# Loading the token records of an expert one expert later, ahead of its weights instead of behind them

## The chip, the cores and the metric

The kernel runs on one core of one Trainium2 chip. The time is the device time of one execution in microseconds (us), the median of the runs named. TensorE (PE) multiplies matrices, VectorE (DVE) and ScalarE (ACT) work element by element, GpSimd (POOL) gathers and scatters rows, and SyncE (SP) issues most transfers. Every transfer, whoever issues it, is moved by the same 16 DMA engines.

## The reference

One layer of a diffusion backbone over 2048 tokens of width 1024: a modulated RMSNorm, an input projection into windowed attention and a gated long convolution, an output projection, and then a mixture of 32 experts. Only that last part is touched. Each token goes to the two best experts of its best group:

```
e_val, e_idx = lax.top_k(jax.nn.softmax(e_logits, axis=-1), TOP_K)
gate = g_val * e_val / jnp.sum(e_val, axis=-1, keepdims=True)
expert = g_idx * EXPERTS_PER_GROUP + e_idx
...
def expert_block(args):
    xb, e = args
    return (jax.nn.silu(xb @ exp_w1[e]) * (xb @ exp_w3[e])) @ exp_w2[e]
...
out = jnp.zeros((n_tok, d), h.dtype).at[tok_sorted].add(y)
```

Each expert has w1 and w3 of 1024x512 and w2 of 512x1024 in float32, 2 MB each, so 6 MB per expert and 192 MB in all.

## The kernel before

The stages before the experts (normalisation, projection, convolution, attention, output projection, router) take the first two thirds of the time. The router stage writes a table in HBM: for each expert, one record (token number and gate) per token that chose it.

`stage6` then goes through the experts 0 to 31 in order. An expert's first 128 tokens are its *main* step (`main`); tokens beyond 128 go in *lots* of 32 (`lot`), which come before the main step. How many there are is read at run time: `span` (L2522, L2523) loads, from the small table `info` in SBUF (part of the tile `lead`), the number of steps of an expert (`many`) and the number of lots before it (`lots`). The steps are numbered through: step n works on record column n of the tile `rec` (`brec`).

Who does what in an expert:

- SP loads w1 and w3 (`load13`, issued at L2557 of the helper, two DMAs of 2 MB into `lead` or `raw`, by parity of the expert), w2 (`load2`, L2561, 2 MB into `w`), and the records (`records`, L2767 for a lot and L2769 for the main step, 1 KB each). All of these go through SP's one hardware queue.
- POOL gathers the token rows of step n+2 during step n: it copies the record column (L2718) and issues the indirect gather into `xg` (L2721). It waits for that record and for PE's transposes of the step (L2813), since `xg` is a single buffer. At the end of a step it adds the results into the output (L2739, for a lot L2730).
- ACT and DVE split the weights of the *next* expert into a high and a low float32r half while PE multiplies with those of this one. ACT's copy of the first quarter of the next w3 (L2645, `w3h`) stands ahead of its copies of the transposed gated values (`gTh`, L2676), for which PE waits before its output product (L2875).
- PE multiplies: L2825 and L2843 in a lot, L2857, L2858, L2863 (hidden), L2875, L2879, L2886 (output) in a main step.

SP's program is one ordered list. In `records` each record waits for the landing of the one before it (`rl` counts them), also for the last; it does not wait for its own landing. `load13` of expert ex+2 waits until the lots of ex are through the first product (`lhm`) and until the low halves of ex have been made (`lo`); `load2` of ex+2 waits for the last output product of ex (`ym`).

Of the kernel before, what the change touches and what calls it, by code (L numbers as in the profile page):

```python
# [42 lines left out]
NE = 32  # L43
# [2386 lines left out]
def stage6(e, g):  # L2430
# [10 lines left out]
    with e.stage(clear=True) as st:  # L2441
# [79 lines left out]
        def span(eng, ex):  # L2521
            many = eng.value_load(info[0:1, 0, bass.ds(ex, 1)], min_val=1, max_val=MANY)  # L2522
            lots = eng.value_load(info[0:1, 1, bass.ds(ex, 1)], min_val=0, max_val=TILES - NE)  # L2523
            return many, lots
# [30 lines left out]
        def load13(eng, ex, par, m):  # L2555
            src = i[("exp_w1", "exp_w3")[m]][0, bass.ds(ex, 1)].rearrange("a (k p) f -> p (a k) f", p=P)
            eng.dma_start(raw13[par][:, m, :, :], src).then_inc(ldw13[m][par], 16)  # L2557

        def load2(eng, ex, par):
            src = i["exp_w2"][0, bass.ds(ex, 1)].rearrange("a (k p) f -> p (a k) f", p=P)  # L2560
            eng.dma_start(w2[par][:, :, :], src).then_inc(ldw2[par], 16)  # L2561
# [193 lines left out]
        @block.sync  # L2755
        def _(sp):
            for b in range(2):
                for m in range(2):
                    sp.sem_inc(ldw13[m][b], 16)
            sp.sem_inc(ldw2[0], 16)  # L2760

            def records(ex, many, lots):
                with sp.If(many > 1):
                    with sp.Fori(0, many - 1) as b:
                        sp.wait_ge(rl, 16 * (lots + ex + b + 1))
                        lot = g.table[bass.ds(ex * CAP + P + b * LOT, LOT), :].unsqueeze(0).broadcast_to([GR, LOT, 2])
                        sp.dma_start(rec[:, bass.ds(lots + ex + b, 1), :].rearrange("p a b -> p (a b)"), lot).then_inc(rl, 16)  # L2767
                sp.wait_ge(rl, 16 * (lots + ex + many))
                sp.dma_start(rec[:, bass.ds(lots + ex + many - 1, 1), :], g.table[bass.ds(ex * CAP, P), :].unsqueeze(1))\  # L2769
                  .then_inc(rl, 16)  # L2770
            first, second, third = span(sp, 0), span(sp, 1), span(sp, 2)
            sp.wait_ge(blank, 1)
            sp.wait_ge(g.last_records, 32)
            sp.sem_inc(passed_s, 1)
            sp.sem_inc(rl, 16)
            sp.sem_inc(lhm, 1)
            records(0, *first)
            records(1, *second)
            records(2, *third)
            sp.wait_ge(g.second_w2, 16)  # L2780
            sp.sem_inc(ldw2[1], 16)

            def next_weights(ex, par, more=True):
                many, lots = span(sp, ex)
                sp.wait_ge(lhm, lots + many)
                sp.sem_inc(passed_s, 1)
                for m in range(2):
                    sp.wait_ge(lo[m], PARTS * (ex + 1))
                    sp.sem_inc(passed_s, 1)
                    load13(sp, ex + 2, par, m)  # L2790
                if more:
                    records(ex + 3, *span(sp, ex + 3))
                sp.wait_ge(ym, 2 * ex + 2)
                sp.sem_inc(passed_s, 1)
                load2(sp, ex + 2, par)
            with sp.Fori(0, NE // 2 - 2) as pair:
                next_weights(2 * pair, 0)
                next_weights(2 * pair + 1, 1)
            next_weights(NE - 4, 0)
            next_weights(NE - 3, 1, False)  # L2800

            total = sp.value_load(info[0:1, 2, NE - 1:NE], min_val=0, max_val=TILES - NE) + NE
            for k in range(2):
                sp.wait_ge(rl, 16 * (total + k + 1))
                sp.dma_start(rec[:, bass.ds(total + k, 1), :], g.table[NE * CAP:NE * CAP + P, :].unsqueeze(1)).then_inc(rl, 16)
# [207 lines left out]
```

## Time and profile before

| what | value |
|---|---|
| median of 3 runs | 2409.44 us (2406.88 to 2416.59) |
| the profiled execution's own time | 2416.59 us, its span 2414.8 us |
| PE busy | 2232.1 us, 92% of the span |
| DVE, ACT, POOL busy | 59%, 51%, 21% |
| DMA | 414.01 MB, mean 171 GB/s |
| the experts' stage | about 1605 to 2415 us of the span |

The profile gives for each engine how long it was busy and what ended its idle time. For SP, "busy" means nothing: what matters there is when it issues each transfer and what it waits for. Views used: waits (who waited for whom), windows (busy time, granted PE clock and DMA share of a stretch), the timeline of one engine, the chain of waits (the work that ended last), and the DMA issues with the time from issue to landing.

### The profile page before, as it was taken

The numbers are of one execution on the slowest core, as the hardware profiler recorded it, in microseconds if no ns is written. First come the engines' busy times: TensorE is split into PE (matmuls) and PEld (weight loads), VectorE is DVE, ScalarE is ACT, GpSimd is POOL, SyncE is SP. The second block draws the span as 40 slices with busy tenths as digits, with TensorE's granted clock in tenths as the row PEclk, the third lists the DMA queues.
The fourth block names the chain that finished last, engine by engine and source line by source line (L and its number), as shares of the span: only waits on it lengthen the run. The fifth ranks groups of instructions, "written<-read, shape, count | busy, mean of one in ns | idle before, by whom it ended". The sixth has DMA issues, their size and how long they took to land. (4 is left out here: it accounts for less than half of the span.)

```text
span 2414.8 us, 43573 instructions
## 1 busy us (share of the span) xinstructions
PE 2232.1 (92%) x15189; PEld 1553.4 (64%) x15190; DVE 1432.3 (59%) x2489; ACT 1232.0 (51%) x2144; POOL 498.3 (21%) x770
## 2 busy tenths in 40 slices
PE   5998999999979999789999999849899999999998
PEld 2335777888846666456666666637666776666775
DVE  4456686232325555555555555448677887666886
ACT  4556322222134444455555555237577777566774
POOL 2672111000011101001222222232222122222122
PEclk8898999999989999899999999969999999999999
DMA  8894222222283542612222221368987998887994
GB/s 295 276 283 137 61 53 78 61 79 70 70 218 91 126 109 73 187 55 62 80 66 79 62 70 62 125 212 291 308 307 256 370 309 292 285 259 238 326 326 150
DMA packets 241969, 414.01 MB, mean 171 GB/s; under 512 B 25572, under 2 KB 129260, under 8 KB 236772
## 3 DMA queue, kind: packets, MB, share of 16 engines
q1 hardware_dynamic: 197904, 354.24, 44.7%
q0 software_dynamic: 18800, 44.71, 7.6%
q10 hardware_dynamic: 25125, 13.18, 2.0%
q8 instruction: 90, 1.47, 0.3%
q14 instruction: 50, 0.40, 0.1%
HBM read 344.83 MB, written 76.85 MB: 175 GB/s over the span
## 5 line engine op out<-in xcount | busy, mean ns | idle before, releaser
L937 PE MATMUL ps_proj<-sb_hTh,sb_winh 128*128 128x512 f32 x576 | 234.0, 406 | 5.4 <-DVE sb_hTl L1089 2.7
L939 PE MATMUL ps_proj<-sb_hTh,sb_winl 128*128 128x512 f32 x576 | 225.2, 391 | 0.0
L938 PE MATMUL ps_proj<-sb_hTl,sb_winh 128*128 128x512 f32 x576 | 225.0, 391 | 0.0
L2237 DVE CUSTOM_DVE_ANT_0 sb_lead<-ps_S,sb_mask 128x640 f32<-128x640 f32 x124 | 102.0, 823 | 88.4 <-PE ps_S L1966 81.9
L2120 ACT ACTIVATE sb_lead<-sb_lead,sb_nm 128x640 f32<-128x640 f32 x128 | 106.3, 830 | 80.2 <-DVE sb_nm L2241 79.0
L1062 ACT COPY sb_rope_or_conv<-ps_proj 128x512 f32<-128x512 f32 x48 | 28.3, 589 | 219.2 <-PE ps_proj L939 144.9
L937 PEld LDWEIGHTS ps_proj<-sb_hTh,sb_winh 128*128 128x128 f32 x576 | 108.7, 189 | 33.4 <-issue 4.1
L2114 ACT COPY sb_lead<-ps_PT 128x512 f32<-128x512 f32 x160 | 89.4, 580 | 74.4 <-PE ps_PT L1958 74.3
L2739 POOL DMA_INDIRECT out<-sb_by,sb_rows_out x32 | 73.2, 2287 | 254.4 <-issue 240.4
L938 PEld LDWEIGHTS ps_proj<-sb_hTl,sb_winh 128*128 128x128 f32 x576 | 108.6, 188 | 25.6 <-issue 4.1
L939 PEld LDWEIGHTS ps_proj<-sb_hTh,sb_winl 128*128 128x128 f32 x576 | 108.6, 188 | 23.3
L1565 DVE TENSOR_TENSOR sb_ab<-sb_ab,ps_gp 128x1024 f32<-128x1024 f32 x64 | 75.3, 1218 | 73.0 <-PE ps_gp L1372 73.0
L1945 PE MATMUL ps_S<-sb_kT,sb_qb 64*128 64x384 f32 x248 | 117.7, 556 | 0.4 <-DVE sb_mx L2237 0.4
L2886 PE MATMUL ps_byp<-sb_w,sb_gT 128*128 128x512 f32 x256 | 115.0, 592 | 0.0
L1145 DVE TENSOR_SCALAR sb_rope_or_conv<-sb_rope_or_conv,sb_cols 128x2048 f32<-128x2048 f32 x11 | 14.8, 1346 | 163.8 <-ACT sb_rope_or_conv L1062 163.8
L2857 PE MATMUL ps_bh<-sb_w1h,sb_bxh 128*128 128x512 f32 x256 | 109.7, 428 | 0.0
L2005 PE MATMUL ps_M<-sb_woh,sb_mixh 128*128 128x512 f32 x256 | 103.9, 406 | 2.0 <-DVE sb_mixl L2323 2.0
L1966 PE MATMUL ps_S<-sb_kT,sb_qb 64*128 64x256 f32 x248 | 90.0, 444 | 16.3 <-DVE sb_mx L2237 11.0
L2609 DVE TENSOR_TENSOR sb_w1l<-sb_w,sb_w1h 128x1024 fp32r<-128x1024 f32 x64 | 75.6, 1222 | 46.7 <-ACT sb_w1h L2682 46.7
L2007 PE MATMUL ps_M<-sb_woh,sb_mixl 128*128 128x512 f32 x256 | 101.3, 396 | 0.0
L2858 PE MATMUL ps_bh<-sb_w1l,sb_bxh 128*128 128x512 f32 x256 | 101.2, 395 | 0.0
L2857 PE MATMUL ps_bh<-sb_w3h,sb_bxh 128*128 128x512 f32 x256 | 101.1, 395 | 0.0
(354 smaller groups left out, 5590.0 us busy)
## 6 DMA issues: line engine op xcount, KB each, us to landing
sb_lead<-in_exp_w SPq DMA_DIRECT2D x32, 2048.0 KB, 14.4
sb_w<-in_exp_w SPq DMA_DIRECT2D x32, 2048.0 KB, 9.1
sb_raw<-in_exp_w SPq DMA_DIRECT2D x32, 2048.0 KB, 14.7
sb_ada<-in_ada_w SPq DMA_DIRECT2D x16, 1536.0 KB, 8.1
scr_filt<-sb_fout SPq DMA_DIRECT2D x128, 128.0 KB, 3.2
sb_yh<-scr_filt SPq DMA_DIRECT2D x64, 256.0 KB, 5.0
scr_hy_in<-sb_hcT ACTq DMA_DIRECT2D x12, 1024.0 KB, 5.5
sb_win<-in_w_in SPq DMA_DIRECT2D x9, 1024.0 KB, 6.0
```

Source lines behind the costliest of these rows:

```text
L937: pe.matmul(mp[:, r % 4, 0:N], a, high[:, k, :], start=(k == 0), stop=False)
L938: pe.matmul(mp[:, r % 4, 0:N], a, low[:, k, :], start=False, stop=False)
L939: ins = pe.matmul(mp[:, r % 4, 0:N], b, high[:, k, :], start=False, stop=(k == KT - 1))
L1945: return pe.matmul(mixer_local if tile.n == 0 and p % 2 else local_of[p % 2], qb[tile.par][0:HD, order[p], :], g.kT[0:HD, order[p] // 4, b ...
L1966: context = pe.matmul(mixer_context if alone and p % 2 else context_of[p % 2], qb[nx.par][HD:2 * HD, order[p], :], g.kT[HD:2 * HD, order[p ...
L2005: pe.matmul(M[:, half, :], mixh[:, k, :], woh[:, k, cs], start=(k == 0), stop=False)
L2007: ins = pe.matmul(M[:, half, :], mixl[:, k, :], woh[:, k, cs], start=False, stop=(k == KT - 1))
L2120: act.activation(pr[:, p, :], pr[:, p, :], ACT.Exp, bias=nm[:, nx.par, p:p + 1], scale=SCALE, accum_out=rsum[:, nx.par, p:p + 1]).then_inc ...
L2237: ve.tensor_tensor_reduce(out=pr[:, p, :], in0=mixer_scores if nx.n == 0 and p % 2 else scores_of[p % 2], in1=mask[:, edge, mask_of[p % 2] ...
L2857: pe.matmul(hp[:, m, :], xh[:, k, :], high[m][:, k, :], start=(k == 0), stop=False)
L2858: pe.matmul(hp[:, m, :], xh[:, k, :], low[m][:, k, :], start=False, stop=False)
L2886: ins = pe.matmul(yp[:, part, :], gT[:, f - SPLIT, :], w2[par][:, f, part * 512:(part + 1) * 512], start=False, stop=(f == FT - 1), skip_g ...
```

## The change

Before, three experts' records were loaded ahead of the loop, and within the turn for expert ex the records of ex+3 were loaded after `load13(ex+2)` and ahead of `load2(ex+2)`. Now two experts' records are loaded ahead of the loop, and the turn for ex begins with the records of ex+2, so that they stand behind `load2(ex+1)` of the turn before and ahead of `load13(ex+2)`. The last two turns, written out after the loop before, are in the loop now.

```diff
-            first, second, third = span(sp, 0), span(sp, 1), span(sp, 2)
+            first, second = span(sp, 0), span(sp, 1)
...
             records(1, *second)
-            records(2, *third)
             sp.wait_ge(g.second_w2, 16)
             sp.sem_inc(ldw2[1], 16)
 
-            def next_weights(ex, par, more=True):
+            def next_weights(ex, par):
+                records(ex + 2, *span(sp, ex + 2))
                 many, lots = span(sp, ex)
                 sp.wait_ge(lhm, lots + many)
                 sp.sem_inc(passed_s, 1)
@@
                     load13(sp, ex + 2, par, m)
-                if more:
-                    records(ex + 3, *span(sp, ex + 3))
                 sp.wait_ge(ym, 2 * ex + 2)
                 sp.sem_inc(passed_s, 1)
                 load2(sp, ex + 2, par)
-            with sp.Fori(0, NE // 2 - 2) as pair:
+            with sp.Fori(0, NE // 2 - 1) as pair:
                 next_weights(2 * pair, 0)
                 next_weights(2 * pair + 1, 1)
-            next_weights(NE - 4, 0)
-            next_weights(NE - 3, 1, False)
```

On SP's list, in the first half of the loop's body, the kernel before has (L2557 is `load13`, L2522 and L2523 read `many` and `lots`, L2767 and L2769 are the records, L2561 is `load2`):

```order
L2557 DMA sb_lead<-in_exp_w1 128x8x512
L2557 DMA sb_lead<-in_exp_w3 128x8x512
L2522 ISA
L2522 TENSOR_LOAD sb_lead
L2522 ISA x2
L2523 ISA
L2523 TENSOR_LOAD sb_lead
L2523 ISA x2
L2763 COMPARE_AND_BRANCH
```

and, after the records of the lots (L2764 is their loop):

```order
L2764 COMPARE_AND_BRANCH
L2763 UNCONDITIONAL_BRANCH
L2768 ISA
L2769 ISA
L2769 REGISTER_ALU
L2769 DMA sb_brec<-scr_table 128x2
L2793 ISA
L2561 DMA sb_w2_0<-in_exp_w2 128x4x1024
```

In the change the same body, from the end of the records on, reads:

```order
L2769 DMA sb_brec<-scr_table 128x2
L2522 ISA
L2522 TENSOR_LOAD sb_lead
L2522 ISA x2
L2523 ISA
L2523 TENSOR_LOAD sb_lead
L2523 ISA x2
L2785 REGISTER_ALU
L2788 ISA
L2557 ISA
L2557 DMA sb_lead<-in_exp_w1 128x8x512
L2557 DMA sb_lead<-in_exp_w3 128x8x512
```

The records have moved from between w3 and w2 to ahead of w1, and between the last record and the next weight load there now stand the two reads of `info`, where before nothing stood but the wait for `ym`. The lists of the other engines keep their order.

## Rows read from the trace of the kernel before

**Rows 1.** Waits, SP from 1600, PE from 1620 us: total us, times, longest.

```profile
SPq L2769 <- DMA sb_brec<-scr_table: 101.5, 16, 12.9
SPq L2767 <- DMA sb_brec<-scr_table: 47.5, 6, 12.1
...
PE ps_btp L2813 <- DMA sb_xg<-scr_xn,sb_rows_in: 10.0, 5, 3.1
```

**Rows 2.** Windows: length, busy of PE, PEld, DVE, ACT, POOL, clock, DMA share, GB/s.

```profile
1699.10:1723.10 24.00, 21.27 (x82) 15.11 (x81) 18.21 (x28) 15.29 (x24) 2.89 (x3) 0.93 0.87 300
1890.10:1909.40 19.30, 19.23 (x83) 14.02 (x81) 16.76 (x26) 13.45 (x21) 4.99 (x3) 1.00 1.04 369
1948.00:1967.80 19.80, 19.73 (x86) 13.99 (x86) 17.33 (x27) 15.23 (x24) 2.88 (x3) 1.00 0.81 273
1683.50:1690.50 7.00, 7.00 (x32) 5.63 (x31) 5.46 (x6) 4.38 (x5) 3.74 (x1) 1.00 0.42 66
1715.00:1718.50 3.50, 3.50 (x11) 2.77 (x12) 2.75 (x8) 2.43 (x8) 0.00 (x0) 0.60 0.78 234
```

**Rows 3.** The chain of waits, 1650 to 1740 us: start, us, what.

```profile
1669.59 15.04 DMA sb_brec<-scr_table
1684.93 2.90 DMA sb_brec<-scr_table
...
1692.55 20.92 DMA sb_raw<-in_exp_w
...
1729.53 7.58 DMA sb_xg<-scr_xn,sb_rows_in
```

**Rows 4.** SP's timeline around expert 5's records: start, us, what.

```profile
1661.18 0.38 SPq L2561 DMA_DIRECT2D sb_w<-in_exp_w  x1
...
1688.13 0.37 SPq L2769 DMA_DIRECT2D sb_brec<-scr_table  x1
1688.77 0.39 SPq L2561 DMA_DIRECT2D sb_w<-in_exp_w  x1
1691.98 4.20 SPq L2557 DMA_DIRECT2D sb_raw<-in_exp_w  x2
```

**Rows 5.** SP's timeline around expert 15's records.

```profile
1934.88 0.38 SPq L2561 DMA_DIRECT2D sb_w<-in_exp_w  x1
1937.30 4.85 SPq L2557 DMA_DIRECT2D sb_raw<-in_exp_w  x2
```

**Rows 6.** w3 of experts 15, 19, 31: SP's issue, then the us to landing.

```profile
1937.85 4.29 SPq L2557 DMA_DIRECT2D sb_raw<-in_exp_w  x1
sb_raw<-in_exp_w SPq DMA_DIRECT2D x1, 2048.0 KB, 20.2
...
2037.52 2.40 SPq L2557 DMA_DIRECT2D sb_raw<-in_exp_w  x1
sb_raw<-in_exp_w SPq DMA_DIRECT2D x1, 2048.0 KB, 20.7
...
2349.91 3.81 SPq L2557 DMA_DIRECT2D sb_raw<-in_exp_w  x1
sb_raw<-in_exp_w SPq DMA_DIRECT2D x1, 2048.0 KB, 19.3
```

**Rows 7.** ACT's timeline: first quarter of w3 of experts 5, 15, 19, 31.

```profile
1713.55 1.04 ACT L2645 CAST sb_w3h<-sb_raw 128x1024 fp32r<-128x1024 f32 x1 [3.89 <-DMA sb_raw<-in_exp_w]
...
1959.79 1.05 ACT L2645 CAST sb_w3h<-sb_raw 128x1024 fp32r<-128x1024 f32 x1 [1.23 <-PE ps_bh L2863]
...
2060.23 1.05 ACT L2645 CAST sb_w3h<-sb_raw 128x1024 fp32r<-128x1024 f32 x1 [1.14 <-PE ps_bh L2863]
...
2370.42 1.05 ACT L2645 CAST sb_w3h<-sb_raw 128x1024 fp32r<-128x1024 f32 x1 [1.23 <-PE ps_bh L2863]
```

**Rows 8.** w2 of expert 3, us to landing; POOL's pick of expert 4's record.

```profile
sb_w<-in_exp_w SPq DMA_DIRECT2D x1, 2048.0 KB, 12.3
...
1673.72 0.18 POOL L2718 COPY sb_rows_in<-sb_brec 128x1 int32 x1 [7.65 <-PE ps_btp L2813]
```

## The prediction

> **What bounds the kernel now.** The page puts PE at 92% of the span. Inside the experts' stage the windows say more: a step of an expert without lots takes 19.30 us, 19.23 of them PE, at a granted clock of 1.00 (2.4 GHz) [rows 2]. The DMA engines are as full there: a share of 1.04 at 369 GB/s. So in such stretches two resources run side by side without slack: PE sets the time, the transfers just keep up. Next I read what SP waits for. It spent 101.5 and 47.5 us waiting for a record to land [rows 1], although a record has 1 KB. The chain of waits shows why: a record issued at 1669.59 was out 15.04 us, the next one, issued at 1684.93 into an empty queue, 2.90 us [rows 3]. The first stood behind 4 MB of weights on SP's queue, the second behind nothing. SP's queue delivers in order.
>
> Then I looked for the places where this reaches PE. There are few. PE waited 10.0 us in five pieces for gathered rows after the start of the stage [rows 1], and the main step of expert 4, 1699.10 to 1723.10, took 24.00 us with PE busy 21.27 [rows 2]. In that step ACT stood 3.89 us before its first copy of expert 5's w3, which landed at 1692.55 + 20.92 = 1713.47 us [rows 3, 7]. That load was late because expert 5 has two lots, so three records: SP issued the last at 1688.13, w2 only at 1688.77 and w1 and w3 from 1691.98 on [rows 4], and meanwhile the DMA share of 1683.5 to 1690.5 was 0.42 at 66 GB/s [rows 2]. This is the stall that the change could be expected to remove.
>
> **The change, part by part.**
>
> *Experts without lots.* Their single record waits only for the record before it, long landed, so SP doesn't stop, before or after. What moves is one more read of `info` between w2 and w1, some 2 us (w2 issued at 1934.88, w1 at 1937.30, with one such read between [rows 5]). Work on the queue hides it: the w2 ahead of it took 12.3 us in such a stretch [rows 8]. Value 0; if the queue were empty it would be 2 us a step, which the share of 1.04 excludes.
>
> *w2 no longer waits for records.* Its issue comes at the end of the main step instead of up to several us later. Nothing waited for w2 before (PE's waits name only gathered rows, besides its one wait for ACT), so this alone gains 0. It only lets the transfers flow on across the end of a step.
>
> *Experts with lots: the records now hold up w1 and w3.* An expert with L lots has L round trips that SP sits out, the first behind a weight load, every further one 3.2 us (1684.93 to 1688.13 [rows 3, 4]) with the queue empty. Before, this hole lay between w3 and the next w2, and when the chain was done w2 followed 0.64 us after the last record's issue [rows 4]. After, the hole lies between w2 and w1 of the same row of transfers, and what follows the last record is the read of `info` and only then w1: 2.4 us [rows 5] to 3.2 us (1688.77 to 1691.98 [rows 4]). The same bytes, the same round trips, and a hole that is 1.8 to 2.6 us longer; I take 2.2. What this costs depends on how long before its use w3 lands. The use is ACT's first copy of w3:
>
> - Expert 5 was late already. w3 now comes 2.2 us later still, and PE with it. The queue's first hole may be smaller than I think, since w2 now joins the queue behind w3 before that has drained, which could save as much as 1 us. Term +2.2 us, between -1 and +4.
> - Expert 15: w3 landed at 1937.85 + 20.2 = 1958.05, used at 1959.79, when ACT had waited for PE, not for the load [rows 6, 7]. Margin 1.7, hole +2.2: +0.5 us, between 0 and 2.
> - Expert 19, three lots: landed at 2037.52 + 20.7 = 2058.2, used at 2060.23 [rows 6, 7]. Margin 2.0. Since expert 15 the queue has not come to rest, and experts 15, 16 and 18 have a lot each, so up to four lengthened holes add up (8.8 us); but w2, which every chain of records held back before, now flows on. I take 4.5 us of lateness: +2.5 us, between 0 and 6.
> - Expert 31: landed at 2349.91 + 19.3 = 2369.2, used at 2370.42 [rows 6, 7]. Margin 1.2, hole +2.2: +1 us, between 0 and 3.
> - The other experts with lots come after a step with lots, which lasts longer than 19.3 us for the same 6 MB, and there the hole is covered. 0, up to +2 together.
>
> *The clock on top.* After the wait of expert 4's step the granted clock was 0.60 over 3.5 us [rows 2], that is, most of it at 1.2 GHz, so that 2.7 us of idle PE became 24.00 - 19.80 = 4.2 us (19.80 is such a step without the wait [rows 2]). That price is in the time of before at expert 5 already; at expert 19 it may come new: +0.5 us, from 0 to 3.
>
> *Gathers.* In a row of lots PE waits for rows whose gather took 7.58 us [rows 3] beside weight loads, and less beside an empty queue. The weight loads shift by a few us against these gathers, to either side: +0.5 us, between -4 and +4 (the whole of what these waits cost is the 10.0 us of rows 1 and the slower clock behind them).
>
> *Is a record late for POOL?* Without lots the record of expert ex+2 is now issued at the start of ex's step and lands behind w2 of ex+1. The worst such row: w2 issued at 1661.18 landed 12.3 us later, at 1673.5, while POOL picked the record at 1673.72 [rows 4, 8]. The record may thus be later than the pick by a us or so. Behind the pick stands the gather, and PE takes its rows at the end of the next main step, some 19 us later; a gather of 7.6 us leaves about 10 us. Value 0.
>
> The Trainium skill ("DMA: Bandwidth & Descriptors", section "Anatomy of one DMA") puts a transfer at about 2.0 us plus its bytes at 436 GB/s, which makes 6.8 us of a 2 MB load. By that estimate w1 and w3 of expert 5, issued after the change at about 1698 us, would land within 12 us, at about 1710, and the stall of that step would go instead of growing. The term of expert 5 would be -4.2 instead of +2.2, and the sum 0.8 us. The trace doesn't agree: for 6 MB the same estimate gives 16.4 us, and w2, w1 and w3 issued from 1688.77 on into an empty queue had landed at 1713.47, after 24.7 us [rows 3, 4].
>
> Sum: 2.2 + 0.5 + 2.5 + 1 + 0.5 + 0.5 = 7.2 us. Against the profiled execution, 2416.59 us, that gives 2423.8. That execution was the slowest of the three; the same step from the median, 2409.44, gives 2416.6, and I forecast 2416 us, +0.3%. A measurement of this kernel can tell about 0.5%, 12 us, from no change.
>
> **The rivals.**
>
> 1. *Nothing moves.* w2's earlier issue makes up for the longer hole, and the margins of 1.2 to 2.0 us hold: -3 to +3 us, 2409. For it: nearly all bytes and round trips are the same, and most experts have slack. Against: the wait at expert 5 has no margin at all.
> 2. *Faster.* The records no longer stand behind 4 MB but behind 2 MB, SP comes free sooner, w3 of expert 5 lands 3 us earlier and its stall of 4.2 us goes; the gathers in rows of lots find a calmer queue and give half of their 10 us back. 2409.44 - 4.2 - 5 = 2400 us. For it: 149 us of SP's waits shrink visibly. Against: the hole in the transfers is not shorter, only elsewhere.
> 3. *Slower, by w1 and w3.* At experts 5, 15, 19 and 31, and where lots follow each other, w3 comes later than its use by more than 3 us each, and each such wait brings the half clock with it: 4 x 4.2 = 17 us, 2426 us. It decides from the point at which the hole grows by more than 4 us over that of before. For it: the hole sits right ahead of the transfer with the tightest deadline, where before it sat ahead of w2, which has slack. Against: margins of some 2 us take off the first part.
>
> By the Trainium skill (same page, "Queues, rings and completion order") each DMA engine takes descriptors of a ring in order, and a semaphore's increment lands after all earlier writes of that engine. The row of the record with its 15.04 us agrees, and it is why I let the record land with the w2 ahead of it.
>
> **How the numbers follow.** My forecast (+3 to +12 us) has 0.42, rival 1 0.27, rival 2 0.12, of which 0.03 below -12 us, rival 3 0.19, of which 0.17 beyond +12 us. That gives faster 0.03, same 0.80, slower 0.17. For the range I take the lower ends together, about -5, and of the upper ends that go together, about +20 us: 2404 to 2430. It holds rivals 1 and most of 3, and leaves out most of rival 2.
>
> **What would show it.** In the profile after: SP's waits for records should fall from 149 us to well below 100, since they stand behind w2 alone; SP's wait for `ym` should grow by as much. The step of expert 4 should still be about 24 to 27 us, ACT's wait for w3 of expert 5 about 6 us instead of 3.89, with small new waits of ACT for w3 of experts 19 and 31. The steps of experts 8 to 13 should stay at 19.30 us. POOL may show picks released by a record's landing, with no wait of PE behind them. I am wrong if the step of expert 4 falls to 20 us (then the hole has closed), or if PE waits at more than four places for ACT's copies of w3 or if PE waits for rows of a gather in steps without lots.

## The result, and the profile after

The changed kernel takes 2430.34 us, the median of 9 runs (2420.69 to 2438.52), against 2415.02 us for the kernel before, also of 9 runs (2406.88 to 2422.40). The ratio is 1.0064, with a 95% interval of 1.0046 to 1.0082: slower by 0.64%. The forecast was +7.2 us or +0.3%, 2416 us, in a range of 2404 to 2430 us. On record are 17 executions of the changed kernel between 2420.69 and 2438.52 us, with a median of 2428.32 us, and one of 12083.08 us, at a granted clock of 0.165, which enters no figure. The pair of profiled executions differs by 11.3 us (2427.88 against 2416.59 us), and it is these two whose rows are compared below. PE runs the same 15189 matrix products in both and is busy 2232.8 us after, 2232.1 us before; in the experts' stage alone it is busy 2.9 us longer, ahead of it 2.2 us less.

Taken from PE's first lot product to the end of the last main step, the experts' stage lasts 792.7 us before (624.1 in main steps, 168.5 in lots) and 806.8 us after (636.8 and 170.0). So 14.1 us come in the stage, of which main steps hold 12.7. The stage starts 2.8 us earlier, at 1609.8 instead of 1612.6 us; over the kernels of this study its start lies anywhere between 1606.4 and 1615.1 us, and in a second profile of the changed kernel at 1608.0, so I don't count it as an effect of the change. PE's line numbers are 4 lower than before: L2809 stands for L2813, L2859 for L2863, L2871 for L2875.

First what SP waits for, from 1600 us on, in the changed kernel: total us, times, longest. L2792 is the wait for the last output product (`ym`).

```profile
SPq L2792 <- PE ps_byp L2882: 268.5, 28, 14.5
SPq L2769 <- DMA sb_brec<-scr_table: 112.4, 15, 16.8
...
SPq L2767 <- DMA sb_brec<-scr_table: 43.0, 6, 12.5
```

SP's wait for records was 149.0 us before [rows 1] and is 155.4 us now. The records stand behind one w2 of 2 MB instead of w1 and w3, yet SP's longest wait for one grew from 12.9 to 16.8 us. What the other engines wait for, from 1620 us on, in the same columns:

```profile
POOL sb_rows_in L2718 <- DMA sb_brec<-scr_table: 42.4, 6, 8.9
...
ACT sb_w3h L2645 <- DMA sb_raw<-in_exp_w: 13.1, 3, 5.0
PE ps_btp L2809 <- DMA sb_xg<-scr_xn,sb_rows_in: 12.7, 6, 3.5
...
PE ps_byp L2871 <- ACT sb_gTh L2676: 10.6, 3, 3.8
```

ACT now waits for w3 three times instead of once [rows 7], and each time PE waits for ACT's copy of the gated values behind it: 10.6 us in three pieces. PE's wait for gathered rows grew by only 2.7 us from the 10.0 us of [rows 1]. The three waits of ACT, for w3 of experts 5, 19 and 31, in its timeline, which are the rows that answer to [rows 7]:

```profile
1711.32 1.04 ACT L2645 CAST sb_w3h<-sb_raw 128x1024 fp32r<-128x1024 f32 x1 [4.44 <-DMA sb_raw<-in_exp_w]
...
2063.93 1.04 ACT L2645 CAST sb_w3h<-sb_raw 128x1024 fp32r<-128x1024 f32 x1 [3.60 <-DMA sb_raw<-in_exp_w]
...
2380.13 1.04 ACT L2645 CAST sb_w3h<-sb_raw 128x1024 fp32r<-128x1024 f32 x1 [5.04 <-DMA sb_raw<-in_exp_w]
```

The windows of the steps concerned (length, busy of PE, PEld, DVE, ACT, POOL, granted clock, DMA share, GB/s), each of the last two followed by the stretch behind its wait:

```profile
1697.80:1722.40 24.60, 21.31 (x105) 15.00 (x108) 17.92 (x27) 13.84 (x22) 2.88 (x3) 0.93 0.78 273
1890.00:1909.30 19.30, 19.23 (x83) 14.02 (x81) 16.78 (x26) 13.47 (x21) 7.32 (x4) 1.00 1.04 364
2048.60:2074.70 26.10, 22.18 (x83) 16.00 (x80) 17.59 (x27) 16.88 (x25) 3.98 (x4) 0.87 0.83 293
2065.30:2074.70 9.40, 9.40 (x22) 5.92 (x22) 7.88 (x13) 5.12 (x12) 0.00 (x0) 0.67 0.51 183
2364.50:2389.60 25.10, 21.29 (x82) 15.13 (x81) 18.01 (x27) 12.66 (x21) 7.52 (x5) 0.93 0.83 292
2381.40:2389.60 8.20, 8.20 (x22) 5.00 (x23) 7.39 (x12) 5.13 (x12) 0.00 (x0) 0.79 0.43 164
```

- The step of expert 4 took 24.57 us, before 24.04 us: +0.5.
- The step of expert 18, in which w3 of expert 19 is needed, took 26.11 us, before 19.46 us: +6.65. PE stood idle for 26.10 - 22.18 = 3.9 us, and behind that the clock was 0.67 over 9.4 us, that is, part of it at 1.2 GHz; PE's busy time in the step grew from 19.4 to 22.2 us.
- The step of expert 30 took 25.09 us, before 19.73 us: +5.36, in the same two parts (clock 0.79 over 8.2 us).
- The steps that neither have lots nor wait for w3 are untouched: 19.30 us at a DMA share of 1.04, as in [rows 2].

These three make +12.5 us of the stage's +14.1. How w3 of expert 19 came to be late stands in SP's timeline (start, us, what; x3 is a group of three issues):

```profile
2021.96 0.37 SPq L2561 DMA_DIRECT2D sb_w<-in_exp_w  x1
2024.35 17.42 SPq L2767 DMA_DIRECT2D sb_brec<-scr_table  x3
2044.34 0.37 SPq L2769 DMA_DIRECT2D sb_brec<-scr_table  x1
2046.73 1.37 SPq L2557 DMA_DIRECT2D sb_raw<-in_exp_w  x2
```

The w2 was issued at 2021.96, the first record 2.39 us behind it, and the second record, which waits for the first, 13.5 us later (2037.87). Then come two round trips of 3.2 us each, and 2.39 us from the last record to w1. The w3 followed at 2047.29, 9.8 us later than before (2037.52, [rows 6]), and landed at 2063.85, 5.6 us later than before (2058.2). The margin there was 2.0 us, so it had to be waited for 3.6 us.

### The profile page after: what moved, and what is told of

Read it like the earlier page. It is cut to its first block and busy times, and to the rows that moved or that the text cites. A ratio compares the mean times of both kernels' runs of the same rounds, so it can differ in the third digit from the quotient of the medians.

```text
span 2426.1 us, 43599 instructions
## 1 busy us (share of the span) xinstructions
PE 2232.8 (92%) x15189; PEld 1553.7 (64%) x15190; DVE 1433.1 (59%) x2489; ACT 1232.4 (51%) x2144; POOL 526.0 (22%) x770
```

## The experiments

Three theories were at hand. **H**: the chain of record round trips, and the read of `info` behind it, hold up w1 and w3, ACT waits for w3, and the clock adds its part. **R**: records that land late release POOL's picks late, and with them the gathers. **W**: w2, issued early, gets in the way of other transfers. A fourth, **V**, was that the stalls of experts 18 and 30 fall differently from one execution to the next and say nothing.

**The read of `info` ahead of the records** (the changed kernel otherwise).

```diff
+                many, lots = span(sp, ex)
                 records(ex + 2, *span(sp, ex + 2))
-                many, lots = span(sp, ex)
```

> The change, with the read of info for the current expert moved ahead of the records, so that w1 follows the last record's issue at once instead of 2.4 us later; the round trips of the records still stand ahead of w1 and w3. Theory H (hole: the transfers stand still between w2 and w1, and w3 misses its use): w3 of experts 5, 19 and 31 lands about 2 us sooner, ACT's waits for w3 fall from 13.1 us to about 7, the steps of experts 4, 18 and 30 shorten by some 2 us each (the last two by more, if the half clock goes too), ratio to before about 1.003. Theory R (rival: records land too late for POOL, gathers start late and collide with w1 and w3): nothing changes, 1.006. Theory W (rival: w2 issued earlier crowds out what is more urgent): nothing changes, 1.006.

Measured: ratio 1.0020 (1.0009 to 1.0032) over the kernel before, median 2416.02 us. Two thirds of the loss are gone, with the same bytes, round trips and order of transfers. Windows of the steps of experts 18 and 30:

```profile
2050.39:2069.85 19.46, 19.39 (x81) 13.89 (x81) 16.23 (x26) 16.61 (x25) 3.25 (x4) 1.00 0.88 295
2359.32:2379.95 20.63, 19.72 (x84) 13.99 (x82) 17.25 (x27) 12.47 (x21) 7.50 (x5) 1.00 0.95 335
```

They are at 19.46 and 20.63 us, at clock 1.00, and expert 4's step is at 21.02 us; ACT's waits for w3 fell from 13.1 to 4.6 us. SP's timeline ahead of expert 19's weights:

```profile
2023.74 0.37 SPq L2561 DMA_DIRECT2D sb_w<-in_exp_w  x1
2027.61 9.99 SPq L2767 DMA_DIRECT2D sb_brec<-scr_table  x3
2040.56 0.36 SPq L2769 DMA_DIRECT2D sb_brec<-scr_table  x1
2041.42 1.01 SPq L2557 DMA_DIRECT2D sb_raw<-in_exp_w  x2
```

From the last record to w1 it is now 0.86 us instead of 2.39, a saving of 1.5 us. But w1 goes out 8.97 us ahead of the start of expert 18's main step (2050.39), against 1.9 us in the changed kernel (2046.73 against 2048.61): 7 us earlier for the 1.5 us of a read. The second record followed the first after 6.1 us instead of 13.5, although the first was issued only 1.5 us later behind its w2 (3.87 us instead of 2.39). I read this as holes that add up over the row of experts with lots (15, 16, 18, 19): a queue that has fallen behind also makes the next record wait longer. POOL's picks were still released by records (expert 18's at 2036.26, after a wait of 5.6 us); theory R had no room for this gain. The +0.20% that is left is not explained: in the profile this version's stage lasts 791.8 us, 0.9 less than before's.

**The read twice** between the last record and w1, in the changed kernel.

```diff
+                span(sp, ex)
                 many, lots = span(sp, ex)
```

> The change, with the read of info between the last record and w1 done twice: the hole ahead of w1 and w3 some 2 us longer than in the change. Theory H: w3 of experts 5, 19, 31 lands about 2 us later again, and that of 15 (1.2 us of margin left in the change) now misses its use by 1 us: ACT's waits for w3 rise from 13.1 to about 20 to 24 us, ratio to before 1.009 to 1.013; the steps of experts 9 to 13, which have one record each, stay at 19.30 us, since the read is covered by w2 on the queue. Rival C (only the round trips of the records hurt, the read is noise): 1.006.

Measured: 1.0103 (1.0088 to 1.0118), 2434.03 us. The steps of experts 18 and 30 took 29.23 and 27.34 us, expert 4's 24.36 us. One such read costs 3.1 and 2.3 us at the two new places, and nothing at the first. With the experiment before it, this gives a slope: 1.0020, 1.0064, 1.0103 with none, one and two reads in the hole. Rival C, by which the read is noise, is out. ACT's waits in this kernel:

```profile
ACT sb_w3h L2645 <- DMA sb_raw<-in_exp_w: 15.1, 4, 5.6
ACT sb_w1h L2645 <- DMA sb_raw<-in_exp_w: 6.6, 2, 5.5
```

Now the wait also reaches w1, which is 2 MB ahead of w3 on the queue. Its waits for w3 alone grew less than the 20 to 24 us expected.

**The place of the change, the distance of before**: records of ex+3 instead of ex+2, ahead of w1 and w3.

```diff
-            def next_weights(ex, par):
-                records(ex + 2, *span(sp, ex + 2))
+            def next_weights(ex, par, more=True):
+                if more:
+                    records(ex + 3, *span(sp, ex + 3))
```

> The place of the change with the distance of before: in the turn for ex the records of ex+3 stand ahead of w1 and w3 of ex+2, and three experts' records are loaded ahead of the loop. Theory H: the hole stays ahead of w1 and w3, but of the expert before: the long chains of experts 5 and 19 now delay w3 of 4 and 18, that of 31 delays w3 of 30. So the stalls move to the steps of experts 3, 17 and 29, and those of 4, 18, 30 go or shrink; ratio about 1.003 to 1.007. Theory R: no record is late for POOL any more, so the time falls back to before, 1.000, with no stall for w3 but that of expert 4. Theory W: like the change, 1.006, with the stalls where they are in it.

Measured: 1.0139 (1.0116 to 1.0162), 2444.66 us, the slowest version that moves the records. The windows of the steps of experts 3, 17 and 29, which were 19.30, 19.82 and 19.30 us before, then of 14:

```profile
1678.18:1703.46 25.28, 21.64 (x82) 15.81 (x81) 17.85 (x27) 13.59 (x21) 4.98 (x3) 0.86 0.83 289
2037.43:2062.25 24.82, 21.27 (x82) 15.12 (x81) 18.45 (x28) 14.04 (x22) 5.01 (x3) 0.93 0.84 291
2362.04:2386.67 24.63, 20.80 (x83) 15.16 (x81) 17.43 (x27) 13.91 (x22) 5.00 (x3) 0.93 1.02 363
1955.07:1983.69 28.62, 22.41 (x83) 15.92 (x82) 18.59 (x28) 15.53 (x24) 2.87 (x3) 0.82 0.91 322
```

The steps of experts 18 and 30 are back at 19.47 and 19.75 us, and stalls stand one expert earlier, where the weights behind the long chains of records are now needed: 3, 17 and 29. No pick waited for a record here, and this kernel is slower than the change. So such stalls need no late pick, which is against R, and it is the place of the chain that costs, not the distance of the change. It went further than H as well: experts 4 (25.48 us) and 14 stall too. One reading is that the chain now stands in a step of 19.3 us whose transfers have no slack; no run here tests it.

**The longer hole ahead of w2**: the kernel before, with one read more between the last record and w2.

```diff
                     records(ex + 3, *span(sp, ex + 3))
+                span(sp, ex)
                 sp.wait_ge(ym, 2 * ex + 2)
```

> The kernel before, with one more read of info (some 1.8 to 2.4 us of SP) between the last record and w2: the hole of before in its old place, as long as in the change. Theory H, if length is what counts wherever the hole stands: w3 lands 2 us later wherever the queue doesn't come to rest; ACT's wait at expert 5 grows from 3.9 to about 6 us, and small ones come at experts 19 and 31, ratio 1.002 to 1.004. Theory H, if the place ahead of w1 and w3 is what counts: within 1 us of before, 1.000. Theories R and W: 1.000.

Measured: 1.0024 (1.0010 to 1.0038), 2419.34 us. The same read, at the old place, costs 0.24%, against 0.4% per read at the new place. Expert 4's step is 24.03 us as before. Expert 18's, as a window:

```profile
2046.22:2067.78 21.56, 19.42 (x84) 13.93 (x80) 15.68 (x25) 15.80 (x24) 2.82 (x3) 1.00 0.86 295
```

It grew by 2.1 us, all of it idle time of PE, at clock 1.00. So the hole lengthened at the old place also costs something at expert 19, without the slower clock. The wait at expert 5 did not grow (3.89 us), though the expectation had it at 6. The ratio fits that expectation, but most of what the profile shows is elsewhere: main steps together take 2.5 us more than before, lots 5.7 us more (expert 21's second 15.11 us instead of 10.59).

**Records issued by POOL**: taken off SP's queue altogether, three experts ahead, the kernel before otherwise.

```diff
             def main(n, ex, par, half, last, lots):
                 gather(n + 2)
+                if not isinstance(ex, int) or ex + 3 < NE:
+                    records_by(pool, ex + 3, *span(pool, ex + 3))
...
                     load13(sp, ex + 2, par, m)
-                if more:
-                    records(ex + 3, *span(sp, ex + 3))
```

`records_by` is `records` with the engine as an argument; POOL also loads the first and the last records.

> Before, with all records issued by POOL through its own queue (those of ex+3 in ex's main step, behind the gather), so that SP only issues weights and never waits for a record. Theory H: no hole in the weights, neither at experts 5, 19, 31 nor elsewhere; ACT's waits for w3 fall to 0 and the 4.2 us of expert 4's step go; against that some 3 to 6 us at the start of the stage, where POOL's first records take longer than SP's: ratio 0.997 to 1.001, and the stage without its start 4 to 8 us shorter than before. Theory R: records come late through the slower queue, PE waits for gathered rows, over 1.003. Theory W: w2 is issued as early as in the change, so what it costs there it costs here, 1.004 to 1.006.

Measured: 1.0117 (1.0092 to 1.0141), 2437.82 us. Waits from 1620 us on:

```profile
POOL sb_brec L2715 <- DMA sb_brec<-scr_table: 65.2, 10, 10.2
...
PE ps_btp L2819 <- DMA sb_xg<-scr_xn,sb_rows_in: 38.9, 8, 11.5
POOL sb_brec L2713 <- DMA sb_brec<-scr_table: 31.7, 7, 11.0
```

ACT's wait for w3 is gone from the list, and expert 4's step fell from 24.04 to 19.81 us: without a chain on SP's queue there is no hole. This is the half that H wanted. But POOL's own queue has the same round trips: it sat in them for 96.9 us and issued gathers late, so that PE waited 38.9 us for rows (expert 6's main step took 28.72 us, expert 18's lot 20.22 us). The hole went to an engine where it costs more. Late records that make PE wait for rows are what R expected of this run, so R's path exists; it is not the one that the change took.

**The change once more**, the same kernel in a second set of runs with a profile of its own.

> The changed kernel once more, for the size of its stalls in a second profiled execution. Theory H with the sizes of the first (19 and 31 at 6.7 and 5.4 us, since a wait of some 4 us brings the slower clock): the steps of experts 4, 18, 30 again above 24, 24 and 24 us, ratio 1.005 to 1.008. Rival V (the sizes are the luck of one execution): at least one of the two steps back within 1 us of before, the other steps as they were.

Measured: 1.0063 (1.0043 to 1.0083), 2426.25 us. The steps of experts 4, 18 and 30 took 24.28, 26.13 and 25.06 us, after 24.57, 26.11 and 25.09, and the stage 806.8 us in both profiles. V is refuted.

**The first record between w1 and w3**, three experts ahead. If the first record's round trip runs beside w3, SP has no hole in front of a weight load for an expert with one lot.

```diff
-                for m in range(2):
-                    sp.wait_ge(lo[m], PARTS * (ex + 1))
-                    sp.sem_inc(passed_s, 1)
-                    load13(sp, ex + 2, par, m)
-                if more:
-                    records(ex + 3, *span(sp, ex + 3))
+                sp.wait_ge(lo[0], PARTS * (ex + 1))
+                sp.sem_inc(passed_s, 1)
+                load13(sp, ex + 2, par, 0)
+                if more:
+                    k = span(sp, ex + 3)
+                    with sp.If(k[0] > 1):
+                        lot_record(ex + 3, *k, 0)
+                sp.wait_ge(lo[1], PARTS * (ex + 1))
+                sp.sem_inc(passed_s, 1)
+                load13(sp, ex + 2, par, 1)
+                if more:
...
+                    last_record(ex + 3, *k)
```

The two parts of `records` are functions of their own here, and further lots' records follow in a loop ahead of the last one.

> Before, with the first lot's record of expert ex+3 issued between w1 and w3 of ex+2 instead of behind both, so that its landing is waited for while w3 is still on the queue: one round trip less without traffic for each expert with lots (none left with one lot, one with two, two with three). Theory H: the hole ahead of w2 of expert 4 shrinks by about 3 us, w3 of 5 lands about 2.5 us sooner, and the 4.2 us of expert 4's step go all but some tenths; ratio 0.997 to 0.999. Rival S (the total of the transfers is the bound there, and a hole only moves idle time): no change, 1.000 within 0.001.

Measured: 0.9987 (0.9975 to 0.9999), 2405.58 us against 2408.58 us: the fastest version. Its SP timeline at expert 19's weights, and the steps of experts 4 and 18 (expert 30's took 19.73 us):

```profile
2019.22 0.38 SPq L2557 DMA_DIRECT2D sb_raw<-in_exp_w  x1
2021.49 0.67 SPq L2774 DMA_DIRECT2D sb_brec<-scr_table  x1
2022.38 1.33 SPq L2557 DMA_DIRECT2D sb_raw<-in_exp_w  x1
2033.75 0.36 SPq L2778 DMA_DIRECT2D sb_brec<-scr_table  x1
2035.22 0.37 SPq L2561 DMA_DIRECT2D sb_w<-in_exp_w  x1
```

```profile
1696.26:1717.10 20.84, 19.75 (x82) 14.00 (x80) 17.43 (x27) 15.16 (x24) 2.89 (x3) 1.00 1.05 373
2042.58:2062.06 19.48, 19.41 (x81) 13.91 (x81) 16.23 (x26) 16.62 (x25) 3.25 (x4) 1.00 0.97 334
```

The record stands between w1 and w3 of expert 19, and w3 goes out at 2022.38, 20.2 us ahead of expert 18's main step, where the changed kernel has 1.3 us. SP waits for its landing until 2033.75, but no weight load is held up in that time, and w2 goes out at 2035.22, 0.2 us after the main step of expert 17 has ended. The step of expert 4, which the kernel before stalls in, fell from 24.04 to 20.84 us, and no new stall came. Main steps give 3.2 us and lots 7.0, so that the stage lasts 782.4 us, 10.2 us less than before. Of the profiled executions this one has a span of 2402.0 us against 2414.8, but the 12 runs say 3 us, so most of the difference between the two traces is not shown to be this edit's. Rival S allowed 0.999, which the interval holds; against it speaks the step of expert 4, 3.2 us shorter for the same bytes.

**A record behind each of w1, w3 and w2** (as the last, but with the chain's end behind w2 where there are two lots or more).

```diff
                 load2(sp, ex + 2, par)
+                if more:
...
+                    with sp.If(k[0] > 2):
+                        last_record(ex + 3, *k)
```

> Before, with one record of ex+3 behind each weight load: the first lot's between w1 and w3, the next behind w3, the rest behind w2, where w2 waits for no record at all any more. No hole is left for up to two lots, one for three. Theory H: no step waits for w3; expert 4's takes 19.8 us; what is left are the waits for gathered rows in rows of lots, which may shift by some us: ratio 0.996 to 0.999. Rival S: 1.000. Rival W (w2 issued early crowds out w1 and w3 or the gathers): above 1.001.

Measured: 0.9998 (0.9988 to 1.0008), 2407.57 us. Expert 4's step took 21.06 us, not the 19.8 expected, and ACT still waited 2.5 us for a w3. The time can't be told from the kernel before, nor clearly from the last. In this version w2 goes out 0.2 to 0.7 us after the end of most main steps, ahead of rows of lots too, and it is not slower than before, so W falls.

**The first record between w3 and w2, the rest behind w2**, three experts ahead.

```diff
                 if more:
-                    records(ex + 3, *span(sp, ex + 3))
+                    k = span(sp, ex + 3)
+                    with sp.If(k[0] > 1):
+                        lot_record(ex + 3, *k, 0)
                 sp.wait_ge(ym, 2 * ex + 2)
                 sp.sem_inc(passed_s, 1)
                 load2(sp, ex + 2, par)
+                if more:
...
+                    last_record(ex + 3, *k)
```

> The change, except that the first lot's record of an expert is issued ahead of w2 (behind w3 of the expert before), so that its landing has been waited for by the time w2 is issued; the other records stay between w2 and w1 as in the change, the last one behind w2, and the read of info still follows it. With one lot no round trip stands ahead of w1 any more, with two lots one, with three two; POOL's picks are as late as in the change wherever there are no lots. Theory H: the stalls of experts 30 (for w3 of 31) and, nearly, of 18 go, w3 of 5 lands about as in before; ratio 1.000 to 1.003. Rival R (late picks and the gathers they push into w1 and w3): experts 18 and 30 stall as in the change, 1.005 to 1.007.

Measured: 1.0016 (1.0005 to 1.0026), 2416.46 us. The stalls of experts 4, 18 and 30 are all gone (19.80, 19.47 and 19.72 us), and the time is still above that of before. In their place there is one new slow step, expert 29's, at 25.05 us instead of 19.30. POOL's timeline shows its cause, PE's the wait:

```profile
2332.60 5.85 POOL L2718 COPY sb_rows_in<-sb_brec 128x1 int32 x1 [9.30 <-DMA sb_brec<-scr_table]
2339.34 1.04 POOL L2721 DMA_INDIRECT sb_xg<-scr_xn,sb_rows_in  x1 [0.88 <-POOL sb_rows_in L2718]
```

```profile
2352.25 1.11 PE L2829 MATMUL ps_btp<-sb_ident,sb_xg 128*128 128x128 f32 x4 [3.51 <-DMA sb_xg<-scr_xn,sb_rows_in]
```

The pick was not only released late by a record: the copy of one column took 5.85 us instead of 0.18 [rows 8]. So the gather left 6.7 us after the pick began, and the rows came 3.5 us too late for PE, in a step without lots. The changed kernel has six late picks as well, and five of them, or the gathers behind them, took 5.6 to 6.7 us; there the rows came in time. POOL and DVE in the changed kernel, at the pick of the same step:

```profile
2340.47 0.18 POOL L2718 COPY sb_rows_in<-sb_brec 128x1 int32 x1 [8.93 <-DMA sb_brec<-scr_table]
2341.53 6.05 POOL L2721 DMA_INDIRECT sb_xg<-scr_xn,sb_rows_in  x1 [0.88 <-POOL sb_rows_in L2718]
```

```profile
2343.17 3.49 DVE L2574 TENSOR_TENSOR sb_w1l<-sb_raw,sb_w1h 128x1024 fp32r<-128x1024 f32 x3
```

The gather ends at 2347.58, 0.9 us behind DVE's group (2346.66).

**Picks late in every main step.** Is it the late landing that makes POOL slow, or what runs beside it? In the kernel before, a further wait puts the pick of each main step behind DVE's first half of `xok`, with the record long there.

```diff
-            def gather(n):
+            def gather(n, late=False):
                 pool.wait_ge(rl, 16 * (n + 2))
+                if late:
+                    pool.wait_ge(xok[0], n)
...
             def main(n, ex, par, half, last, lots):
-                gather(n + 2)
+                gather(n + 2, late=True)
```

> The kernel before, with one more wait in POOL's gather of a main step: it waits for the first half of the low parts of the turned rows (xok), which DVE finishes some 3.5 us after PE's transposes, and so picks the record late in every main step, with the record landed long before. In the kernels where a record landed late, the instruction behind such a pick took 5 to 6.8 us instead of 1.04. Theory P (the place beside DVE): that time belongs to the stretch in which DVE makes three low parts of w1 (3.49 us) back to back; every main step then shows it: POOL's gather takes 4 to 7 us in nearly all 28 main steps inside the loop, ends where DVE's group ends, and its rows land 10 to 14 us after the issue instead of 7; PE may wait for rows at one to three more places, 2410 to 2420 us. Theory Q (the late landing itself, a queue just emptied or a full one): a record landed long ago leaves the gather at about 1.04 us and its landing at about 7 us, only 3.5 us later than before; time unchanged, 2405 to 2415 us.

Measured: 1.0267 (1.0250 to 1.0284), 2473.91 us. POOL's rows and then DVE's, in the same stretch:

```profile
1904.61 3.77 POOL L2720 COPY sb_rows_in<-sb_brec 128x1 int32 x1 [11.40 <-DVE sb_bxl L2588]
1909.27 1.04 POOL L2723 DMA_INDIRECT sb_xg<-scr_xn,sb_rows_in  x1 [0.89 <-POOL sb_rows_in L2720]
```

```profile
1903.65 1.28 DVE L2588 TENSOR_TENSOR sb_bxl<-sb_bxf,sb_bxh 128x512 fp32r<-128x512 f32 x2
1904.85 3.49 DVE L2574 TENSOR_TENSOR sb_w1l<-sb_raw,sb_w1h 128x1024 fp32r<-128x1024 f32 x3
```

POOL's copy began at 1904.61 and ended at 1908.38; DVE's row of subtractions, all with both inputs in SBUF, ended at 1908.34, and the copy stayed out over the four of them that followed each other, not over one alone. The median of the 51 picks from 1620 us on is 3.76 us, their shortest 0.18 us. Theory P of this run holds as to the place beside DVE: no record was late at these picks. It was wrong in two things. It is the copy that waits, the gather behind it takes its 1.04 us; and the price was 64 us, not 10 at most, since PE waited 64.3 us in 15 pieces for rows, in the lots that follow a main step (expert 8's first lot took 14.78 us, expert 21's 14.87). The Trainium skill ("SBUF — State Buffer", section "Who interferes with whom") describes the port pair that DVE and GpSimd share as an exclusive lock: a DVE operation with two SBUF inputs and a GpSimd operation that reads SBUF keep each other out, and the later one waits fully. The ends of the two instructions, 0.04 us apart, agree; here the wait lasted over a whole row of DVE operations. No run took the DVE operations away, so that it is this lock is read from the ends and the page.

## Why the prediction was wrong in size, and where its mechanism held

The measured time lies just above the range. Of the 13.7 us between 2416.6 and 2430.34 us, 5.6 are the kernel before, whose median of 9 runs is 2415.02 us where the forecast started from 2409.44, and 8.1 are the change: +15.3 us instead of +7.2. The first part is the luck of three runs; the second is not, since the interval begins at +0.46%, 11 us.

The path was right: late records, late w3, ACT's copy, PE's wait, the clock. The step that failed is the size of the hole: "The same bytes, the same round trips, and a hole that is 1.8 to 2.6 us longer; I take 2.2". Counted in us from the start of the main step two experts earlier, first in the kernel before, then in the change:

| expert | w2 of the expert before it issued | its w1 issued | its w3 landed |
|---|---|---|---|
| 5 | 9.0, 0.7 | 12.2, 17.1 | 33.7, 34.2 |
| 15 | 6.2, 0.7 | 8.6, 14.5 | 29.3, 30.3 |
| 19 | 13.2, 0.7 | 15.6, 25.5 | 36.9, 42.6 |
| 31 | 7.3, 0.7 | 10.1, 17.5 | 29.9, 34.8 |

For expert 31, SP's timeline in the kernel before, then in the change:

```profile
2346.15 0.37 SPq L2769 DMA_DIRECT2D sb_brec<-scr_table  x1
2346.63 0.38 SPq L2561 DMA_DIRECT2D sb_w<-in_exp_w  x1
2349.42 4.29 SPq L2557 DMA_DIRECT2D sb_raw<-in_exp_w  x2
```

```profile
2345.93 0.37 SPq L2561 DMA_DIRECT2D sb_w<-in_exp_w  x1
2348.34 0.67 SPq L2767 DMA_DIRECT2D sb_brec<-scr_table  x1
2360.36 0.37 SPq L2769 DMA_DIRECT2D sb_brec<-scr_table  x1
2362.74 2.06 SPq L2557 DMA_DIRECT2D sb_raw<-in_exp_w  x2
```

Before, SP sat out the records' landings partly while PE still worked on the product that w2 waits for (`ym`); then w2, w1 and w3 went out together. In the change w2 goes out as soon as `ym` allows, and only then does the first record start; it waits for w2 to land (12.0 us here, 13.5 us at expert 19), and w1 waits for it. So w1 goes out 4.9 to 9.9 us later, not 2.2. A part comes back, because w2 is no longer on the queue with them: w3 of these experts landed 15.3 to 16.8 us after its issue instead of 19.3 to 20.9. What is left is 0.5, 1.0, 5.8 and 4.9 us.

- **Experts without lots, 0**: right. Their steps stay at 19.30 us and DMA share 1.04.
- **w2 no longer waits for records, 0**: right as a gain of nothing. It had the side that the working left out: the first record now stands behind w2 in flight, and SP waited up to 16.8 us for one. The expectation that SP's waits for records would fall well below 100 us failed: they rose to 155.4 us. SP's wait for `ym` grew, from 121.9 to 268.5 us, but not in their place. The working also said that PE's waits name only gathered rows besides the one for ACT; they name DVE too, 10.3 us in the lots. None is for w2.
- **Expert 5, +2.2 (-1 to 4)**: too high, it was +0.5 us. ACT's wait went from 3.89 to 4.44 us. The w3 was issued at 1694.64 and landed at 1711.24, 16.6 us later, where before it took 20.9 us: the hole is longer, but the queue is emptier when w1 and w3 come, as the text allowed. The Trainium skill's estimate ("DMA: Bandwidth & Descriptors", "Anatomy of one DMA") had the stall there gone; the step took 24.57 us, and the measurement decides against it. That section's figure is fitted on transfers that GpSimd issues, while SP issues these.
- **Expert 15, +0.5**: measured 0 (19.80 to 19.79 us), inside its bounds; w3 came 1.0 us later there, within its margin of 1.7.
- **Expert 19, +2.5 and +0.5 for the clock (0 to 6 and 0 to 3)**: the step of the sum that failed first. It measured +6.65 us, 3.9 us of idle PE and 2.8 us of slower clock: inside its bounds, at more than twice its size. The lateness that I took, 4.5 us, was 5.6 us. That it is this hole which sets it is shown by the versions with the read ahead (19.46 us) and twice (29.23 us).
- **Expert 31, +1 (0 to 3)**: the second, +5.36 us, above its upper bound. I put one hole lengthened by 2.2 us against one margin of 1.2 us. The w3 landed at 2380.06, 10.9 us later than before (2369.2). ACT came to it 5.9 us later than before (idle from 2375.09 instead of 2369.19), so the load itself had lost 5.0 us, not 2.2: 7.5 us at its issue (2363.30), less 2.5 us of shorter flight (16.8 instead of 19.3 us), as above. With the read ahead of the records the step took 20.63 us, with the first record ahead of w2 19.72.
- **The clock on top**: its rate stood in [rows 2], where 2.7 us of idle PE became 4.2 us. By it, 3.9 and 3.8 us of idle are 6.1 and 5.9 us, and 6.65 and 5.36 us were measured. I gave the two new waits together 0.5 us of clock. Against the forecast, experts 19 and 31 cost 8.0 us more (12.0 against 4.0): 3.9 us of that are clock, 4.1 us longer idle.
- **Gathers, +0.5 (-4 to 4)**: lots cost +1.5 us together (expert 8's second lot +2.4, expert 22's -1.5), in the range.
- **A late pick, 0**: right in its value for this kernel, wrong in its working. The six picks waited 42.4 us for records and PE did not wait for their rows. But I had left 10 us over behind a gather of 7.6 us. The gather issued at 2341.53 landed 13.0 us later instead of about 7, at 2354.5, and PE took the rows at 2356.82: 2.3 us were left. In the version with the first record ahead of w2 they were gone, and 3.5 more.

Of the rivals, the third comes closest: slower, by waits for w3 that bring the half clock, 2426 us. It had four places at 4.2 us; there were two new ones at 5.4 and 6.7 us. The point from which it decides (a hole that grows by more than 4 us) was passed at all four experts if w1's issue is counted, 4.9 to 9.9 us, and at two in w3's landing, 5.8 and 4.9 us. At expert 19 it was to be read from the rows, four lengthened holes in a row, and the forecast counted them at half. Its chance of 0.19 was small for what the rows said. Rival 1 lacked exactly these margins; rival 2's first part is real (the version with the first record between w1 and w3 has it), but the change does not reach it.

Two things stay open. Of the 14 us between the profiled stages about 12.5 are shown in three steps; 1.5 us lie in lots. The two profiles of the change agree there in sum (170.0 us) and to 0.6 us in the single lot, but of the kernel before there is one profile, so it is not shown whether the lots' 1.5 us belong to the change. And the version with the read ahead of the records still loses 0.20% in its runs, with no step that shows it.

## What to carry to other kernels

A chain of small loads, each of which waits for the one before, let the queue run empty here: ask which transfer stands right behind it, and put there the one with the most time before its use, or nothing but bytes that already flow (a first record between two weight loads was hidden; the same record behind them was not). When a wait is moved in a list, ask not only how long it is but when it can begin: here it began only once w2 was out, where before part of it had passed under PE's work. When a wait is likely to appear on TensorE, price it with the clock: in this kernel 2.7 to 3.9 us of idle cost 4.2 to 6.7 us. And a few instructions on the sync engine between two DMAs are not free when the queue is empty: here each read of two values from SBUF, 1.5 us of SP, was worth 0.4% of the kernel ahead of w1, and 0.24% ahead of w2.

## What the runs showed of the hardware

- GpSimd's copy of 128x1 values takes 0.18 us, 3.77 us when it starts while VectorE runs a row of subtractions with both inputs in SBUF, and 5.85 us in one case; it ends with them (1908.38 against 1908.34 us). In the change it was the gather's issue, at 2341.53, that took 6.05 us instead of 1.04, and its rows landed 13.0 us after it instead of 7.0.
- A record of 1 KB behind 2 MB of w2 let the next one go after 13.5 us where w3 had gone out 6.5 us ahead of that w2, after 6.1 us where it had gone out 11.2 us ahead, and after 3.2 us with nothing ahead of it.
- Behind an idle time of 3.9 us TensorE's granted clock was 0.67 over 9.4 us, so part of it at 1.2 GHz; in a step with 2.1 us of idle (the longer hole ahead of w2) it was 1.00 throughout.
- SP's queue delivered its weight loads in the order of their issue: all 90 in the stage of the kernel before whose landing the profile has.
